# Forgetting attention on Trainium2: another order for the memory's norm, the unit pieces and x_k, and a second half of w_out by tiles

## The reference

```python
fx_out = forgetting_attention(fq, fk, fv, flf)      # 8 heads of 64, causal, softmax over
                                                    # q.k * 64**-0.5 + c[q] - c[k]
x = x + concat([ml_out, fx_out]) @ w_out            # 1024 x 1024
# cross_attention(rmsnorm(x, ln_x), rmsnorm(mem, ln_mem), w_xq, w_xkv, w_xo), 4 heads of 256:
memn = rmsnorm(mem, ln_mem)                         # 256 x 1024
k, v = split(memn @ w_xkv)                          # x_k, x_v
q = rmsnorm(x, ln_x) @ w_xq                         # x_heads
```

## Time and profile before

| | |
|---|---|
| median of 3 runs | 2898.06 us (2897.51 to 2898.32) |
| the profiled execution: its time, its span | 2903.7 us, 2901.9 us |
| TensorE busy | 2781.6 us, 96% of the span |
| DVE, ACT, POOL busy | 1031.3, 922.9, 581.4 us |
| granted TensorE clock, mean | 0.984 of full |
| mean of one w_hi conversion (ACT), one w_lo (POOL) | 1.055, 2.447 us |

### The profile page before, as it was taken

How to read it: one execution, slowest core, us unless ns; L and a number is a source line. 1 busy time by engine, 2 the same in 40 slices (tenths; PEclk the granted TensorE clock), 3 DMA queues, 4 the chain that set the end, 5 groups by cost and what they waited for, 6 DMA issues and landing times.

```text
span 2901.9 us, 34459 instructions
## 1 busy us (share of the span) xinstructions
PE 2781.6 (96%) x13636; PEld 2283.7 (79%) x13636; DVE 1031.3 (36%) x1292; ACT 922.9 (32%) x1469; POOL 581.4 (20%) x246
## 2 busy tenths in 40 slices
PE   7999999999999999999998998999999999999999
PEld 6677788898888887777676776877687888888887
DVE  3444423653322223734424664222324213022123
ACT  4455531112222124433434554243423212121122
POOL 1000012211222222321111222251012222222221
PEclk9899999999999999999999998999999999999999
DMA  3000001111111113221111213230011111111112
GB/s 122 13 13 13 14 22 51 45 51 37 44 49 50 48 47 127 87 68 37 44 37 56 52 42 114 82 116 29 22 51 39 49 51 49 46 52 51 44 51 87
DMA packets 49918, 152.54 MB, mean 53 GB/s; under 512 B 13108, under 2 KB 13364, under 8 KB 49032
## 3 DMA queue, kind: packets, MB, share of 16 engines
q1 hardware_dynamic: 44848, 126.01, 13.9%
q10 hardware_dynamic: 4952, 24.82, 2.2%
HBM read 135.95 MB, written 10.67 MB: 51 GB/s over the span
## 4 chain that ended last, share of the span: by engine, by line
PE 83%; issue 6%; DVE 5%; ACT 3%; POOL 2%; DMA 1%; ACTq 0%; POOLq 0%; DVEq 0%; SPq 0%
PE ps L557 45%; PE ps L638 16%; PE ps L760 3%; PE ps L657 3%; PE ps L1069 2%; PE ps L731 2%; PE ps L1027 1%; POOL w_lo L475 1%; PE ps L749 1%; PE ps L1208 1%; PE ps L1021 1%; PE ps L616 1%; DVE fx_tl L2475 1%; PE ps L1127 1%; PE ps L1106 1%
## 5 line engine op out<-in xcount | busy, mean ns | idle before, releaser
L475 POOL TENSOR_TENSOR w_lo<-w_raw,w_hi 128x1024 fp32r<-128x1024 f32 x213 | 521.2, 2447 | 2028.0 <-ACT w_hi L1308 2028.0
L557 PE MATMUL ps<-A_hi,w_hi 128*128 128x512 f32 (+1 forms) x1920 | 550.0, 373 | 6.8 <-DVE mla_tmp L2146 1.5
L557 PE MATMUL ps<-A_lo,w_hi 128*128 128x512 f32 (+1 forms) x1920 | 545.3, 370 | 0.0
L557 PE MATMUL ps<-A_hi,w_lo 128*128 128x512 f32 (+1 forms) x1920 | 544.8, 370 | 0.0
L1308 ACT ACTIVATE w_hi<-w_raw 128x1024 fp32r<-128x1024 f32 x213 | 224.6, 1055 | 556.9 <-PE ps L638 382.8
L557 PEld LDWEIGHTS ps<-A_hi,w_hi 128*128 128x128 f32 x1920 | 342.2, 189 | 71.1 <-issue 7.7
L557 PEld LDWEIGHTS ps<-A_lo,w_hi 128*128 128x128 f32 x1920 | 343.7, 189 | 61.7
L557 PEld LDWEIGHTS ps<-A_hi,w_lo 128*128 128x128 f32 x1920 | 343.3, 188 | 61.6
L2538 DVE TENSOR_TENSOR X<-ps,X 128x512 f32<-128x512 f32 x96 | 66.4, 691 | 391.9 <-PE ps L638 338.1
L638 PE MATMUL ps<-w_lo,U_hi 128*128 128x512 f32 x448 | 174.3, 389 | 0.0
L638 PE MATMUL ps<-w_hi,U_lo 128*128 128x512 f32 x448 | 174.3, 389 | 0.0
(11 more groups left out here) (424 smaller groups left out, 4067.6 us busy)
## 6 DMA issues: line engine op xcount, KB each, us to landing
w_raw<-in_units SPq DMA_DIRECT2D x203, 512.0 KB, 3.5
X<-in_x ACTq DMA_DIRECT2D x4, 1024.0 KB, 12.3
X<-in_x ACTq DMA_DIRECT2D x1, 4096.0 KB, 15.2
x_spill<-X ACTq DMA_DIRECT2D x1, 4096.0 KB, 12.2
X<-x_spill ACTq DMA_DIRECT2D x1, 4096.0 KB, 14.0
out<-lnf_xn SPq DMA_DIRECT2D x8, 512.0 KB, 2.6
w_raw<-in_units SPq DMA_DIRECT2D x12, 256.0 KB, 2.6
negm_bc<-negm_rows ACTq DMA_DIRECT2D x4, 512.0 KB, 3.6
```

Source lines behind the costliest of these rows:

```text
L475: nc.gpsimd.tensor_tensor(w_lo[:, slot, :], w_raw[:, slot, :], w_hi[:, slot, :].bitcast(F32), ALU.subtract).then_inc(w_lo_ready, 1)
L557: last = nc.tensor.matmul(out, w[:, slot, o:o + m], v[:, k, cols] if k is not None else v[:, cols], start=(first and j == 0 and q == 0), s ...
```

## The change

1. In `SEGMENTS` x_k comes before w_out, and its eight units run inside the last steps of the attention, one in each step from head 6, s=1 on, and the last after the attention (`fx_fill`). The keys x_kT get a place of their own.
2. Pieces of a half are moved up by one step and lie whole at the end of a step: piece 0 goes ahead of head 0. Evacuations of halves come in s=1 and s=3 instead of s=0 and s=2, the next unit's conversion in s=1.
3. The memory's two tiles are normalised before the stage, and transposed between halves 0 and 1. Its split form is loaded a first time for x_k, over the last rows of A (`mem_hi_a`, `mem_lo_a`), when unit 7 has been used, and a second time for x_v as before.
4. SP's, ACT's, POOL's and DVE's orders follow, with `inverse(6)` and `inverse(7)` among the loads of the x_k units, and `normalised` among POOL's.
5. The second half of w_out is `sweep_tiles`, with `lnx` in the order of ln2 (`LNX_PAIRS`): tiles 0 to 4 in the sweep, 5 behind it, 6 and 7 behind x_v's first two units. x_v's loops are written out.

```diff
-    ("w_out", 2, (1024,) * 4),
-    ("x_k", 2, (1024,) * 4),
+    ("x_k", 1, (1024,) * 8),
+    ("w_out", 1, (1024,) * 8),
...
@@ SP, fx_loads
+                for h in range(6):
+                    next_load(n0 + 3 + h)
+                    copies(2 * h + 3)
+                    copies(2 * h + 4)
                     inverse(h)
+                next_load(n0 + 9)
+                sp.wait_ge(unit_done, n0 + 8)
+                sp.wait_ge(mem_moved, 32)
+                sp.dma_start(mem_hi_a[:, :, :].bitcast(F32), memh_d).then_inc(mem_moved, 16)
+                sp.dma_start(mem_lo_a[:, :, :].bitcast(F32), meml_d).then_inc(mem_moved, 16)
+                copies(15)
+                for n in range(n0 + 10, n0 + 13):
+                    next_load(n)
+                inverse(6)
+                for n in range(n0 + 13, n0 + 17):
+                    next_load(n)
+                inverse(7)
+                next_load(n0 + 17)
...
@@ POOL
+            for h in range(7):
                 if h >= 1:
+                    normalised(h - 1, n0 + h + 3)
+                low(n0 + h + 3, (n0 + h + 3) % 2)
+                if h >= 1:
+                    value_low(h + 1)
+            for n in range(n0 + 10, n0 + 14):
+                low(n, n % 2)
+            normalised(6, n0 + 14)
+            for n in range(n0 + 14, n0 + 18):
+                low(n, n % 2)
+            normalised(7, n0 + 18)
+            e = FIRST["w_out"] + 4
+            for n in range(n0 + 18, e):
+                low(n, n % 2)
+            low_held(e, wout_hi, wout_lo)
...
@@ TensorE
+            def fx_fill(piece):
+                if piece <= FX_FILL:                       # FX_FILL = 25
+                    fx_half(3 + piece // 2, 7, 12 * (piece % 2), 12 * (piece % 2) + 12)
+                else:
+                    q = piece - FX_FILL - 1
+                    n = FIRST["x_k"] + q
+                    pe.wait_ge(w_lo_ready, n + 1)
+                    if q == 0:
+                        pe.wait_ge(fx["q_lo"], 4 * HEADS)
+                        pe.wait_ge(mem_moved, 64)
+                    else:
+                        pe.wait_ge(xa["k"], q)
+                    passes([(ps[:, 7, 0:256], slice(0, 256))], n % 2, 0, range(KT), P, mem_hi_a, mem_lo_a).then_inc(unit_done, 1)
             fx_half(0, 0, 0, 24)
+            mem_tile(0)
+            mem_tile(1)
             fx_half(1, 1, 0, 24)
-            norm("lnmem", mem_t_[1], 2, (2, 3), lambda o: pe.wait_ge(sw["fx_v"], 2 * o + 6))
...
             fx_scores(0, 0)
+            fx_fill(0)
...
-                    if m < 2 * HEADS:
-                        fx_half(m, 7, f0, f0 + 6)
                     if j >= 3:
                         fx_turn(h, s, (3,))
-                    if m < 2 * HEADS:
-                        fx_half(m, 7, f0 + 6, f0 + 12)
+                    fx_fill(4 * h + s + 1)
             fx_values(7, 3)
+            fx_fill(4 * HEADS + 1)
...
-            sweep("w_out", "mix", A_hi, A_lo, META, sw["w_out"], free=fx_read)
+            sweep_half("w_out", "mix", A_hi, A_lo, META, range(ST), fx_read)
+            sweep_tiles(FIRST["w_out"] + 4, wout_hi, wout_lo, A_hi, A_lo, META, lambda o: pe.wait_ge(sw["w_out"], TILES[o] + 1),
+                        lambda o: lnx_tile(o - 3) if o >= 3 else None)
+            lnx_tile(5)
+            for hb in range(2):
+                pe.wait_ge(xa["v"], hb + 1)
                 for kp in range(4):
+                    n = n0 + 4 * hb + kp
+                    sweep_unit(n, n % 2, kp, mem_hi, mem_lo, 0, tiles=range(2), signal=False, bank=2)
+                    if hb == 0 and kp < 2:
+                        lnx_tile(6 + kp)
...
@@ ACT
+            def x_key(q):
+                n = FIRST["x_k"] + q
+                act.wait_ge(unit_done, n + 1)
+                fn(x_kT[:, q, :], ps[:, 7, 0:256], ACT.Copy).then_inc(xa["k"], 1)
+                feed(n + 2, n % 2, (n + 2) // 2)
             fx_high(0)
+            lnmem.high(0)
+            lnmem.high(1)
             fx_high(1)
...
-                    if s in (0, 2) and 3 <= m < 2 * HEADS:
-                        fx_high(m)
+                    if k % 2 and 3 + k // 2 < 2 * HEADS:
+                        fx_high(3 + k // 2)
+                    if k > FX_FILL:
+                        x_key(k - FX_FILL - 1)
...
-                    if s == 2 and h <= 6:
+                    if s == 1 and h <= 6:
                         feed(n0 + h + 3, (n0 + h + 3) % 2, (n0 + h + 3) // 2)
...
+            for o in range(4, ST):
+                lnx.high(o)
             n0 = FIRST["x_v"]
...
@@ DVE
+            lnmem.xn()
+            lnmem.xn()
             fx_low_parts(0)
+            lnmem.low(0)
+            lnmem.low(1)
             fx_low_parts(1)
...
-                    if s in (0, 2) and 3 <= m < 2 * HEADS:
-                        fx_low_parts(m)
+                    if k % 2 and 3 + k // 2 < 2 * HEADS:
+                        fx_low_parts(3 + k // 2)
```

More of the change, by code:

```diff
@@ L82 @@
 LN2_PAIRS = (2, 3, 2, 3, 0, 1, 0, 1)
+LNX_PAIRS = (2, 3, 2, 3, 0, 2, 0, 2)
 def ffn_pair(u):
@@ L447, in _ @@
                     fx_loads()
+                elif name == "x_k":
+                    continue
                 elif name == "w_out":
-                    for n in range(n0 + 3, n0 + 8):
+                    for n in range(n0 + 2, n0 + 8):
                         sp.wait_ge(w_lo_ready, n - 1)
@@ L1160, in fx_read @@
                     pe.wait_ge(fx["pl"], FX_CHUNKS * HEADS)
-                if o == 2:
+                if o == 6:
                     pe.wait_ge(fx["o"], 4 * HEADS)
-            sweep("w_out", "mix", A_hi, A_lo, META, sw["w_out"], free=fx_read)
[L1167 to L1175, removed]
@@ L1177, in _ @@
[L1177 to L1187 removed]
+                if o == 7:
+                    pe.wait_ge(xa["k"], KT)
@@ L1882, in _ @@
-            n0 = FIRST["x_k"]
-            with act.Fori(0, 2) as i, chain.loop(i, 2, 2):
-                for u in range(4):
-                    after(n0, i, 4, u)
-                    settle()
-                    fn(x_kT[:, ds(i * 4 + u, 1), :].rearrange("p a c -> p (a c)"), ps[:, 4 + u % 2, 0:256], ACT.Identity)\
-                        .then_inc(xa["k"], 1)
-                    if u % 2:
-                        lnx_high(i, u // 2, u // 2)
-                    else:
-                        lnx_stats(i, 4 + u // 2)
+            act.wait_ge(fx["pv"], 4 * HEADS)
@@ new lines, in _ @@
+            feed_half(n0 + 4, wout_hi)
+            feed_last(n0 + 4)
+            lnx = Norm("lnx", lambda t: X[:, t, :], lnx_t, A_hi, TILES, 32, META, LNX_PAIRS,
+                       ready=lambda o: act.wait_ge(sw["w_out"], ST + o + 1))
+            for o in range(ST):
+                if o >= 4:
+                    lnx.high(o - 4)
+                if o == ST - 1:
+                    after(n0, 0, 8, 6)
+                lnx.stats()
+            after(n0, 0, 8, 7)
+            for o in range(4, ST):
+                lnx.high(o)
@@ L1893, in _ @@
             n0 = FIRST["x_v"]
-            with act.Fori(0, 2) as i:
+            for hb in range(2):
                 for kp in range(4):
-                    after(n0, i, 4, kp)
-                    if kp % 2:
-                        lnx_high(i, 4 + kp // 2, kp // 2)
-                    if kp == 3:
-                        settle()
-                        fn(x_v[:, :, ds(i * HB, HB)], ps[:, 2:4, :], ACT.Identity).then_inc(xa["v"], 1)
+                    after(n0 + 4 * hb, 0, 4, kp)
+                fn(x_v[:, :, hb * HB:hb * HB + HB], ps[:, 2:4, :], ACT.Identity).then_inc(xa["v"], 1)
```

141 lines of the change are left out of this document (45 added, 96 removed).

## The result

The kernel after takes 2917.66 us in the median of 5 runs (2910.58 to 2919.78), the kernel before 2898.32 in its 5 (2897.51 to 2904.59): ratio 1.0056, 95% interval 1.0037 to 1.0074. So it is slower, by some 16 us, where 2878.6 was forecast. The profiled execution took 2919.36 us for a span of 2917.6, which is 15.7 more than before's span.

A forecast was written before the change was run, and what follows sets the result against it. TensorE's matmul order, 83% of the last-ending chain, was taken as the bound. With w_out starting 2.3 us later and 21.8 us saved from there to x_heads, -19.5 us gave a 2878.6 us median; range 2867 to 2890, 8 in 10.

The forecast's parts named there:

- SP, which the moved conversion meets: Heads 1 to 5: unit load behind the inverses' store reaches ACT's earlier conversion late, 1.1 us a head, bounds 0.3 and 2.6.
- s - 8.6: ACT's lateness per head in us, s being the time from the inverses' store to SP's next issue, taken as 9.7.
- The start of the stage: Norm and transposes of the memory moved: first attention transposes at 1554.3 instead of 1559.63, 5.3 us earlier.
- A head without SP's part: A steady attention head's four steps sum to 26.65 us instead of 28.77, 2.1 less.
- The memory: Head 6: x_k's first unit waits 9.8 us for the memory's two loads, plus about 1.3 us of slow restart.
- Unit 13: Head 7, s=1: the fourteenth unit's load stands behind inverse(6), so TensorE waits 1.9 us.
- w_out's second unit: Start of w_out: the second unit's load hangs on inverse(7), 1.8 us late (0 to 3.5).
- x_v: From x_v's first units to x_heads 33.5 us, including 4.8 idle before the third unit and a 2.70 us evacuation wait.
- its own signs: Wrong if heads stay above 28.5 us, the memory wait is under 5 or over 14, or w_out to x_heads not 126-132.
- C: Rival, slower: SP held at the inverse store in eight places, not faster from a 12.1 us store, 2905 at 13; chance 0.04.
- A: Rival, faster: SP's waits hide, the memory lands when wanted and stores are short, 20.3 us go, 2858 us; chance 0.12.
- B: Rival: moved pieces don't shorten a head, the period stays 28.77 us, 2890 us in all; chance 0.12.

The follow-up runs named there:

- e2: The changed kernel with SP issuing each next unit's load ahead of the inverses' store, heads 0 to 5; 2891.73 us, ratio 0.9970 to the kernel before.
- e7: The changed kernel with the inverses stored in 128 pieces of 32 bytes instead of 1024 of 4, heads scaled wrongly; 2875.07 us, ratio 0.9913.
- e4: The changed kernel with all unit loads ahead of the inverses on SP, memory pair between head 5's store and its wait; 2885.69 us, ratio 0.9945.
- e5: e4 with the memory's two loads issued by ACT instead of SP; 2881.07 us, ratio 0.9929.
- e9: e6 with the memory's two loads ahead of the sixth head's inverse store on SP, later copies and load behind it; 2874.39 us, ratio 0.9904.
- e6: e4 with x_v's second unit ahead of the last two lnx transposes, its third converted ahead of their copies; 2875.40 us, ratio 0.9905.
- e8: e4 with the edits of both e5 and e6; 2872.92 us, ratio 0.9906.
- e3: The changed kernel without SP's wait for the inverses' store, fx_inv loaded from elsewhere, heads scaled wrongly; 2901.87 us, ratio 1.0006.

## Why the prediction was wrong

**The step that failed** is the term "SP, which the moved conversion meets": 1.1 us in each of heads 1 to 5, with bounds 0.3 and 2.6. The mechanism was named rightly and e2 confirms its place; its size was off. It measured 5.2 us a head: 32.08 us in the mean, against 26.84 with the load ahead of the store. Three parts, from the five heads of after:
- the store took 9.96, 10.37, 10.45, 11.02 and 11.08 us, mean 10.58, where 9.7 was taken: +0.9. The prediction lowered the mean of eight because two short stores (8.88, 9.45) had no copies just ahead. That reason doesn't hold: head 5's store has them, and took 9.14 us in the kernel before and 8.85 in after. The five of heads 0 to 4 in the kernel before had a mean of 10.8, and those stand where the conversion meets them. What makes head 5's short is not shown.
- the unit's load took 6.48, 5.01, 6.60, 6.09 and 5.12 us, mean 5.86, where 3.6 was taken: +2.3. That 3.6 is the median of all 34 loads. The five that stood behind an inverse in the kernel before are in its own trace (DMA issues, 1575 to 1735):

```profile
w_raw<-in_units SPq DMA_DIRECT2D x5, 512.0 KB, 5.1
```

 By the prediction's own formula the two make s - 8.6 + 2.3 = 4.2 us a head instead of 1.1. The kernel before's rows alone would have given 10.8 - 8.6 + 1.6 = 3.8 (its five loads have a mean of 5.2); the 0.7 us by which the load was slower still in after are not explained.
- TensorE's restart: 5.2 us a head is about 1 us above those 4.2. By the windows 3.3 of it are idle time and 2.0 longer matmuls at the lower clock. The prediction priced a slow restart behind the one 10 us wait, and none behind waits of 3 to 4 us.

Five heads: 160.38 for 138.75 us. Head 0 took 26.40 for 26.9.

**The other steps.** The start of the stage: right as an instant, by luck; 1.6 us too long as a stretch. The spill and the low parts of half 2 came when forecast (24.6 us after the first matmul, for 24.3), but piece 0, which fills the wait, was given 4.1 us, "at the lower clock at first". It took 5.25, all of it at half clock (1.2 GHz), behind a wait of 4.35:

```profile
1549.01:1554.26 5.25, 5.25 (x12) 3.99 (x13) 2.11 (x2) 2.63 (x5) 2.17 (x1) 0.50 0.51 135
```

A head without SP's part: right (26.84 for 26.65, in e2 and e7). The memory: 10.16 us for 9.8, from two errors that nearly cancel. The pair was issued 9.9 us into head 6 for 10.7, and took 10.7 us to land for 9.4. The prediction counted the store in the issue alone; against e7, with the quick store, the issue is 3.1 us later and the pair 1.8 us slower, and the wait 10.16 instead of 5.20. Unit 13: 3.60 us for 1.9, the same two terms (store 9.44, load 5.96). w_out's second unit: 2.94 for 1.8. w_out's second half by tiles: right (93.27 to 93.83 us in e4 and e7, where the second unit is in time, for 93.6). x_v: 39.89 for 33.5. Its 4.8 us wait was right (4.48) and x_v's evacuation nearly (2.06 for 2.70); too small were the two tiles (2.71 idle for 0.4) and the units behind the waits, at a window clock of 0.91. Of the 6.4 us, an estimate from these numbers, 1.8 are idle time (11.7 for some 9.9) and 4.6 longer matmuls (28.2 us busy for some 23.6). By its own signs the prediction failed twice, a head above 28.5 us and w_out to x_heads in 137.9 us, not in 126 to 132; the sign of the one long wait held.

**The rivals.** C, the slower one, named the right place, SP held at the store, but hung it on a store of more than 12.1 us; none took more than 11.1. The loss came by what lands behind the store, which C held fixed. A (waits hide) is refuted by after's waits of 10.16, 3.60 and 2.94 us, B (a head stays at 28.77) by the 26.84 of a head with the load ahead. The chance of 0.04 for C was far too small for a term that entered eight places and whose bounds had been taken from the store alone.

**What stays open.** How much of the pair's landing in after is the store and how much the loads beside it: in e5 7.6 and 12.5 us beside both, in e7 4.8 and 8.5, in e9, ahead of the store, 4.9 and 7.2. And no run has the inverses stored in order with larger pieces; that is where e7 points. The best kernels here that compute the whole reference are e6, e8 and e9, 0.9904 to 0.9906 of the kernel before, and not told apart.

## What to carry to other kernels

When an operation is moved in a queue, price the transfer that it now meets by the rows of transfers in that same place (behind the same store), not by the median of its kind; and count a lateness in each place that it enters, with a slow restart of TensorE on top. A wait that a small scattered store causes doesn't belong to the engine that waits: it moves to whatever is issued behind the pieces, so put the urgent load ahead, or make the pieces fewer. A good change can be a loss by one queue's order: moving one load ahead of one store turned it (e2).

## What the runs showed of the hardware that was not expected

**4 KB in 1024 pieces.** The store took 10.4 us in 4-byte pieces and 1.4 in 128 of 32 bytes, and in e3 a load of 512 KB issued 1.07 us behind it was ready only after 13.2 us. Behind the pair of 1 MB loads the store itself took 15.2 us (e9).

**VectorE beside GpSimd.** VectorE's and GpSimd's timelines of after, ahead of the 2.71 us wait in x_v:

```profile
1910.72 2.28 DVE L2035 SCALAR_TENSOR_TENSOR lnx_xn<-X,stat,lnx_g 128x1024 f32<-128x1024 f32 x1 [0.18 <-PE ps L610]
...
1913.11 3.39 DVE L2035 SCALAR_TENSOR_TENSOR lnx_xn<-X,stat,lnx_g 128x1024 f32<-128x1024 f32 x1
```

```profile
1909.55 2.37 POOL L497 TENSOR_TENSOR w_lo<-w_raw,w_hi 128x1024 fp32r<-128x1024 f32 x1 [43.38 <-ACT w_hi L1344]
1913.02 2.40 POOL L497 TENSOR_TENSOR w_lo<-w_raw,w_hi 128x1024 fp32r<-128x1024 f32 x1 [1.09 <-ACT w_hi L1344]
```

Alone the same operation takes 1.28 us (1.28 to 1.29 for the six tiles before it in after, while GpSimd was idle). Here both end 1.08 us behind the end of a GpSimd operation: 1911.92 and 1913.00, 1915.42 and 1916.50. The Trainium skill (SBUF — State Buffer, SBUF: two separate sides) says that a VectorE operation with two inputs in SBUF and a GpSimd operation take a shared port one after the other; these rows agree, and e2, e4, e6 and e7 have the same two durations within 0.01 us. The 3.1 us that the two took more than twice 1.28 cover the 2.3 which x_v's tiles waited more than forecast.

**The clock behind short waits.** Behind waits of 2.7 to 4.4 us part of each head of after ran at 1.2 instead of 2.4 GHz, and the mean granted clock of a whole head fell to 0.90 to 0.95; with no wait above 0.42 us (e2) it stayed at 1.00. In five heads this made 9.9 us of longer matmuls. Shorter waits can do it too: in e3 heads with one wait of 2.02, 2.22 and 2.29 us had 0.94, but one with 2.47 us had 1.00, as had the one with 1.05.
